# Stick-breaking attention on TensorE: the transposes of tile m-5 put ahead of the scores of tile m+3

## The chip, the cores and the metric

The program runs on one core of a Trainium2 chip. The metric is the device time of one execution in microseconds (us); the number that counts is the median over runs.

## What is computed

One inference step of an encoder layer for a prompt of 2048 rows and 32 sample rows, model width 1024. The part that matters here is the prompt's attention, 8 heads of width 64, strictly causal, with stick-breaking weights in place of a softmax:

```python
def stick_breaking_block(q_blk, q_pos, k, v, k_pos):
    z = jnp.einsum("bqhd,bkhd->bhqk", q_blk, k) * SB_SCALE
    mask = k_pos[None, :] < q_pos[:, None]
    log_1mb = jnp.where(mask, jax.nn.log_sigmoid(-z), 0.0)
    log_a = jax.nn.log_sigmoid(z) + lax.cumsum(log_1mb, axis=3, reverse=True) - log_1mb
    a = jnp.where(mask, jnp.exp(log_a), 0.0)
    return jnp.einsum("bhqk,bkhd->bqhd", a, v)
```

So the weight of key s for query t is sigmoid(z[t,s]) times the product of sigmoid(-z[t,j]) over the keys j between s and t. Ahead of it stand the conditioning, a layer norm, the projections and a pooling branch; behind it the output projection, two layer norms, a SwiGLU block and the sample rows.

## The kernel before

The kernel is one long program with hand-written queues for TensorE (`pe`), ScalarE (`act`), VectorE (`v`), GpSimd (`pool`) and the DMA queue (`sp`). Each engine runs its own list in order, and semaphores join them. No planner is in it: the order around the change is the order of the loops as they are written.

The attention stage goes over 8 heads. A head has ten units: query block b of 512 rows (0 to 3) against key block kc of 512 columns, from kc = b down to 0. The unit with kc == b is the diagonal one. With D for a diagonal unit and F for a full one, a head is D, D F, D F F, D F F F. A unit has four tiles, so there are 320 tiles; tile m = 4u + j belongs to unit u. On the score side, a tile is 128 query rows (j) by 512 key columns; in a diagonal unit tile j has only 128(j+1) columns. On the weight side, tile k = 4u + kt is one block of 128 keys (kt), transposed for up to four groups of query rows; in a diagonal unit kt has 4 - kt of them. These are the steps on a tile, with their lines:

- TensorE, `scores(m)`: two f16 matmuls into PSUM bank m % 4 (line 2211). From m = 4 on they wait until scan m-4 has freed the bank. In some units, j = 0 has also sixteen matmuls of a conditioning piece (line 2209).
- ScalarE, `plus(m)`, for a pair of tiles: the first sigmoid, into the buffer of weights C_A of the unit, of which there are three (line 1172). It waits for the scores of both tiles.
- ScalarE, `minus(m)`, for the same pair: the second sigmoid, in PSUM (line 1184).
- VectorE, `scan(m)`: the running product over the keys from right to left, out of PSUM into a row buffer (line 1707, on the diagonal 1704).
- GpSimd, `product(m)`: weights times the scan's result (line 880), on the diagonal behind a mask (line 876).
- TensorE, `turn_weights(k)`: up to four 128x128 f32 transposes into bank 4 + k % 2 (line 2234). With kt == 0 it waits for the product of the unit's last tile; from k = 2 on it waits until tile k-2 has been copied out.
- The copy of tile k out of PSUM into C_AT: ScalarE makes three of four (line 1195), VectorE the one with k % 4 == 1 (line 1725). VectorE's list has it at m = k + 6, behind scan(m), so the copy of tile 4i+1 stands behind scan 4i+7.
- TensorE, `weigh(k)`: weights times values, f32, into bank 6 or 7 (line 2250), for two tiles in every other pass of the loop.

At the end of each query block ScalarE (`head_low`, line 1202) and VectorE (line 1734) take the result out, and in odd heads GpSimd splits it into two f16 halves (lines 888 and 890, between two products). In even heads ScalarE and VectorE also split the pooling branch (`pool_high`, line 1210, and line 1742). ScalarE's list per unit is, with v the unit of the sigmoids: second sigmoid of tiles 2 and 3 of unit v-1, copy of tile 0 of unit v-2, first and second sigmoid of tiles 0 and 1 of unit v, copy of tile 2 of unit v-2, first sigmoid of tiles 2 and 3 of unit v, copy of tile 3 of unit v-2, and the second sigmoid of tiles 2 and 3 of unit v. `copied(k)` gives the semaphore and the count that stand for the copy of tile k:

```python
def copied(k):
    by_dve = (k + 3) // 4
    return (at_dve, by_dve) if k % 4 == 1 else (at_act, k + 1 - by_dve)
```

TensorE's list for the stage is the loop at line 2278: pass m has scores(m+3), then turn_weights(m-5), in every even pass weigh(m-8) and weigh(m-7), and at the very end the first matmuls of the output projection. Waits of the DMA queue on `z_mm` (scores done), `at_mm` (transposes done) and `av_mm` (weighed) release the loads of the next heads' q, k and v and of the conditioning pieces.

Of the kernel before, what the change touches and what calls it, by code (L numbers as in the profile page):

```python
# [57 lines left out]
def encoder_step(nc, x_prompt, x_sample, cache_k, cache_v, state_pool, c_prompt, c_sample,  # L58
# [5 lines left out]
    with ctx:  # L64
# [240 lines left out]
        NTILE = 4 * NU * NH  # L305

        def tile_of(m):
            u, j = m // 4, m % 4
            b, kc = UNITS[u % NU]
            return u, u // NU, b, kc, j, (j + 1) * P if kc == b else BLK  # L310
# [5 lines left out]
# [3 lines that stand above are left out]
# [1741 lines left out]
        def _(pe):  # L2060
# [136 lines left out]
            def scores(m):  # L2197
                u, h, b, kc, j, w = tile_of(m)
                e = h % 2
                qt = (4 * b + j) * P  # L2200
                if m % (4 * NU) == 0:
                    pe.wait_ge(head_in[e], 64 * (h // 2) + 64)
                if m >= 4:
                    pe.wait_ge(scan_set, m - 3)
                if j == 0 and u in ADA_AT:
                    pe.wait_ge(ada_in, 16 * (ADA_AT.index(u) + 1))
                    for d in range(KD):
                        at = TS * (d % 4)
                        pe.matmul(ps[at:at + TS, 0, 256:512], CT[:, d, :], C_ADA[:, d, :], start=(d < 4), stop=(d >= 4))
                for half in range(2):  # L2210
                    mm = pe.matmul(ps[:, m % 4, 0:w], C_Q[e][:, qt:qt + P], C_K[e][:, half, BLK * kc:BLK * kc + w],  # L2211
                                   start=(half == 0), stop=(half == 1))
                mm.then_inc(z_mm, 1)

            def turn_weights(k):
                u, h, b, kc, kt, w = tile_of(k)
                j0 = kt if kc == b else 0
                if kt == 0:
                    pe.wait_ge(prod_set, k + 4)
                if k >= 2:  # L2220
                    pe.wait_ge(*copied(k - 2))
                if kt == 1 and u in ADA_AT:
                    pe.wait_ge(mod_new, ADA_AT.index(u) + 1)
                    for q in range(2):
                        pe.matmul(ps[:, 4 + k % 2, 2 * q:2 * q + 2], MOD_ROW[:, q * P:(q + 1) * P], SEL,
                                  start=True, stop=True)
                if k == FIN_TURN:
                    pe.wait_ge(fin_max, 1)
                    pe.transpose(ps[0:5, 4 + k % 2, 0:P], small[:, 86:91], ident[:, :])
                if k == FIN_SPREAD:  # L2230
                    pe.wait_ge(fin_max, 2)
                    pe.matmul(ps[:, 4 + k % 2, 0:5], ones_r[0:5, :], TOP_DIAG[0:5, 0:5], start=True, stop=True)
                for j in range(j0, 4):
                    mm = pe.transpose(ps[:, 4 + k % 2, j * P:(j + 1) * P], C_A[u % 3][:, j, kt * P:(kt + 1) * P],  # L2234
                                      ident[:, :])
                mm.then_inc(at_mm, 1)

            def weigh(k):
                u, h, b, kc, kt, w = tile_of(k)
                e, r = h % 2, HD * (kt % 2)  # L2240
                j0 = kt * P if kc == b else 0
                pe.wait_ge(*copied(k))
                if k % (4 * NU) == 0:
                    pe.wait_ge(v_in[e], 16 * (h // 2) + 16)
                if kc == b and kt == 0 and 4 * h + b >= 2:
                    pe.wait_ge(o_scaled, 4 * h + b - 1)
                if kc == b and kt == 1:
                    pe.matmul(ps[HD:P, 6 + b % 2, 0:P], C_TRI[:, 0:HD], ident_b[:, :], start=True, stop=False,
                              skip_group_check=True)
                pe.matmul(ps[r:r + HD, 6 + b % 2, j0:BLK], C_V[e][:, 4 * kc + kt, :], C_AT[k % 4][:, j0:BLK],  # L2250
                          start=(kc == b and kt < 2), stop=(kc == 0 and kt >= 2),
                          skip_group_check=True).then_inc(av_mm, 1)

            def first_mix(k):
                pe.wait_ge(wo_hi, k + 1)
                pe.wait_ge(wo_lo, k + 1)
                if k == 0:
                    pe.wait_ge(o_split, 13)
                    pe.wait_ge(scan_set, NTILE - 2)
                for n in range(2):  # L2260
                    for xh, wh in TERMS:
                        mm = pe.matmul(ps[:, n, :], hidden_t[:, k, xh, tile_cols(0)], D_WO[k][:, wh, 512 * n:512 * (n + 1)],
                                       start=(k == 0 and (xh, wh) == (0, 0)),
                                       stop=(k == KD - 1 and (xh, wh) == TERMS[-1]))
                if k == KD - 1:
                    mm.then_inc(d_mm, 1)
# [9 lines left out]
            pe.wait_ge(mix_max, 2)  # L2276
            pe.matmul(ps[:, 7, 256:257], ones_r[0:1, :], TOP_DIAG[0:1, 0:1], start=True, stop=True).then_inc(mix_ar, 1)
            for m in range(NTILE + 7):
                if m + 3 < NTILE:
                    scores(m + 3)  # L2280
                if m == 5:
                    pe.wait_ge(kvt_out, 40)
                    pe.wait_ge(mix_set, 1)
                if 5 <= m < NTILE + 5:
                    turn_weights(m - 5)
                if m >= 8 and m % 2 == 0:
                    weigh(m - 8)
                    weigh(m - 7)
                if m >= NTILE + 1:
                    first_mix(m - NTILE - 1)  # L2290
# [258 lines left out]
```

## Time and profile before

| | |
|---|---|
| median of 3 runs | 2576.05 us (2575.98 to 2579.04) |
| the profiled execution's own time | 2579.84 us |
| its span | 2578.1 us |
| busy over the span | TensorE matmuls 2432.3 us (94%), weight loads 1347.5 (52%), VectorE 1415.5 (55%), ScalarE 1017.5 (39%), GpSimd 866.3 (34%) |
| TensorE clock granted, mean | 0.979 of full speed |
| attention stage | from about 484 to 1004 us of the span |

The profile is one execution, recorded by the hardware. The first view gives each engine's busy time; matmuls are pipelined, so neighbours overlap a little in it. A wait is idle time of an engine ahead of an instruction, put down to what released it. In a timeline, one line is one or several instructions of a kind in a row: start, duration up to the end of the last, engine, line of the program, operation, output and inputs, and in brackets the idle time before it. PE is TensorE's matmuls, PEld its weight loads, DVE is VectorE, ACT is ScalarE, POOL is GpSimd.

### The profile page before, as it was taken

The numbers are of one execution on the slowest core, as the hardware profiler recorded it, in microseconds if no ns is written. First come the engines' busy times: TensorE is split into PE (matmuls) and PEld (weight loads), VectorE is DVE, ScalarE is ACT, GpSimd is POOL, SyncE is SP. The second block draws the span as 40 slices with busy tenths as digits, with TensorE's granted clock in tenths as the row PEclk, the third lists the DMA queues.
The fourth block names the chain that finished last, engine by engine and source line by source line (L and its number), as shares of the span: only waits on it lengthen the run. The fifth ranks groups of instructions, "written<-read, shape, count | busy, mean of one in ns | idle before, by whom it ended". The sixth has DMA issues, their size and how long they took to land.

```text
span 2578.1 us, 36259 instructions
## 1 busy us (share of the span) xinstructions
PE 2432.3 (94%) x14328; PEld 1347.5 (52%) x14328; DVE 1415.5 (55%) x1861; ACT 1017.5 (39%) x1555; POOL 866.3 (34%) x1029
## 2 busy tenths in 40 slices
PE   4899899899999889999999999999999999999998
PEld 2445455444444444454565664345666544688733
DVE  4747665488888887889655553405333202433214
ACT  1522233499999994334444443102222200133200
POOL 1300000277777773324555556501111240111100
PEclk8899999899999999999999999999999999999999
DMA  7315868432332112222566666654544445566555
GB/s 250 101 50 172 279 235 270 127 99 82 99 97 68 34 66 98 78 98 77 166 198 195 190 204 224 237 183 155 162 161 135 136 135 181 160 222 200 187 164 167
DMA packets 216387, 395.63 MB, mean 153 GB/s; under 512 B 30189, under 2 KB 152365, under 8 KB 207642
## 3 DMA queue, kind: packets, MB, share of 16 engines
q1 hardware_dynamic: 199226, 331.45, 40.0%
q10 hardware_dynamic: 16992, 61.87, 7.8%
q8 instruction: 113, 1.85, 0.3%
q14 instruction: 56, 0.46, 0.1%
HBM read 302.97 MB, written 90.30 MB: 153 GB/s over the span
## 4 chain that ended last, share of the span: by engine, by line
PE 59%; DVE 9%; ACT 4%; DMA 3%; issue 3%; POOL 3%; SPq 0%; DVEq 0%; POOLq 0%; ACTq 0%
PE ps L2455 20%; PE ps L2495 15%; PE ps L2424 12%; PE ps L2359 3%; DMA dn_dram<-work 3%; DVE work L1707 2%; PE ps L2234 2%; PE ps L2250 2%; PE ps L2211 2%; POOL work L880 2%; ACT ps L1184 1%; ACT work L1172 1%; DVE work L1864 1%; DVE work L1704 1%; DVE work L1454 1%
## 5 line engine op out<-in xcount | busy, mean ns | idle before, releaser
L2455 PE MATMUL ps<-hidden_t,work 128*128 128x384 f16 (+1 forms) x3696 | 515.4, 303 | 2.2 <-ACT work L1305 1.1
L2495 PE MATMUL ps<-work 128*128 128x512 f16 x2244 | 472.6, 380 | 7.5 <-DVE work L1962 4.9
L2455 PEld LDWEIGHTS ps<-hidden_t,work 128*128 128x128 f16 x3696 | 361.3, 98 | 156.3 <-ACT work L1305 1.7
L2118 PE MATMUL ps<-hidden_t,work 128*128 128x416 f16 x1920 | 351.7, 343 | 14.3 <-DVE hidden_t L1472 9.8
L880 POOL TENSOR_TENSOR work<-work 128x512 f32<-128x512 f32 (+2 forms) x320 | 307.7, 964 | 134.4 <-DVE work L1707 76.4
L2424 PE MATMUL ps<-hidden_t,work 128*128 128x384 f16 x2112 | 347.4, 328 | 4.1 <-DVE work L1919 4.1
L2495 PEld LDWEIGHTS ps<-work 128*128 128x128 f16 x2244 | 206.6, 98 | 272.9 <-issue 28.6
L2424 PEld LDWEIGHTS ps<-hidden_t,work 128*128 128x128 f16 x2112 | 207.5, 98 | 144.2 <-issue 9.6
L2118 PEld LDWEIGHTS ps<-hidden_t,work 128*128 128x128 f16 x1920 | 189.7, 99 | 163.6 <-issue 16.1
L1707 DVE TENSOR_TENSOR_SCAN work<-ps,work 128x512 f32<-128x512 f32 x192 | 237.3, 1270 | 26.8 <-ACT ps L1184 25.7
L841 POOL TENSOR_TENSOR work<-work,col 128x1 f32<-128x1 f32 x68 | 33.2, 489 | 582.7 <-DVE work L1457 582.7
L945 POOL TENSOR_TENSOR work<-work 128x384 f16<-128x384 f32 (+1 forms) x88 | 75.2, 859 | 418.6 <-ACT work L1325 418.6
L2211 PE MATMUL ps<-work 128*128 128x512 f16 (+3 forms) x640 | 175.2, 357 | 37.1 <-DVE work L1707 29.6
L1979 DVE TENSOR_TENSOR work<-ps,work 128x1024 f32<-128x1024 f32 (+1 forms) x17 | 20.8, 1224 | 311.3 <-PE ps L2495 310.3
L2234 PE MATMUL ps<-ident,work 128*128 128x128 f32 x1088 | 178.9, 281 | 11.9 <-POOL work L880 6.9
L2234 PEld LDWEIGHTS ps<-ident,work 128*128 128x128 f32 x1088 | 132.5, 144 | 79.0 <-DVE work L1725 32.8
L1172 ACT ACTIVATE work<-ps,col 128x1024 f32<-128x1024 f32 (+1 forms) x160 | 165.5, 1034 | 8.5 <-PE ps L2211 6.9
L1184 ACT ACTIVATE ps<-ps,col 128x1024 f32<-128x1024 f32 (+1 forms) x160 | 161.3, 1008 | 2.2
L2250 PE MATMUL ps<-work 128*64 128x512 f32 (+3 forms) x640 | 160.8, 559 | 0.0
L1195 ACT ACTIVATE work<-ps,col 128x512 f32<-128x512 f32 (+2 forms) x240 | 148.5, 619 | 27.4 <-PE ps L2234 24.8
L2359 PE MATMUL ps<-work,hidden_t 128*128 128x512 f16 x720 | 159.2, 381 | 0.0
L1291 ACT ACTIVATE work<-ps 128x384 f32<-128x384 f32 (+1 forms) x44 | 19.6, 445 | 319.0 <-PE ps L2455 319.0
(243 smaller groups left out, 2691.6 us busy)
## 6 DMA issues: line engine op xcount, KB each, us to landing
work<-dn_dram ACTq DMA_DIRECT2D x96, 512.0 KB, 3.6
work<-gs_dram SPq DMA_DIRECT2D x88, 512.0 KB, 4.1
work<-gs_dram SPq DMA_DIRECT2D x44, 768.0 KB, 4.3
work<-in_w_ada SPq DMA_DIRECT2D x24, 1024.0 KB, 5.3
work<-in_w_gu SPq DMA_DIRECT2D x46, 512.0 KB, 7.0
work<-in_w_gu SPq DMA_DIRECT2D x22, 1024.0 KB, 6.0
gs_dram<-work SPq DMA_DIRECT2D x22, 1024.0 KB, 5.7
gs_dram<-work SPq DMA_DIRECT2D x66, 256.0 KB, 2.4
```

The source lines that it names most:

```text
L880: pool.tensor_tensor(a[:, 0:n], a[:, 0:n], PRJ[:, j, BLK * kc + 1:BLK * kc + n + 1], ALU.mult).then_inc(prod_set, 1)
L1172: act.activation(C_A[u % 3][:, j:j + 2, 0:n], ps[:, z:z + 2, 0:n], ACT.Sigmoid, scale=c1(C_Z + 2 * (h // 2) + 1)).then_inc(be_set, 1)
L1184: act.activation(ps[:, z:z + 2, 0:n], ps[:, z:z + 2, 0:n], ACT.Sigmoid, scale=c1(C_Z + 2 * (h // 2))).then_inc(sg_set, 1)
L1707: v.tensor_tensor_scan(row, ps[:, m % 4, w - 1::-1], row, PRJ[:, j, at + w:at + w + 1], ALU.mult, ALU.bypass).then_inc(scan_set, 1)
L2118: mm = pe.matmul(ps[:, blk, 0:PB], B_HL[s][:, wh * KD * P + k * P:wh * KD * P + (k + 1) * P], hidden_t[:, k, xh, PB * blk:PB * (blk + 1)], ...
L2211: mm = pe.matmul(ps[:, m % 4, 0:w], C_Q[e][:, qt:qt + P], C_K[e][:, half, BLK * kc:BLK * kc + w], start=(half == 0), stop=(half == 1))
L2234: mm = pe.transpose(ps[:, 4 + k % 2, j * P:(j + 1) * P], C_A[u % 3][:, j, kt * P:(kt + 1) * P], ident[:, :])
L2250: pe.matmul(ps[r:r + HD, 6 + b % 2, j0:BLK], C_V[e][:, 4 * kc + kt, :], C_AT[k % 4][:, j0:BLK], start=(kc == b and kt < 2), stop=(kc == 0 ...
L2359: mm = pe.matmul(ps[:, 2 * s + n, :], hidden_t[:, k, xh, tile_cols(t)], D_WO[k][:, wh, 512 * n:512 * (n + 1)], start=(k == 0 and (xh, wh) ...
L2424: mm = pe.matmul(ps[:, 2 * blk + w, 0:width], E_GHL[s][:, wh, w, k, :], hidden_t[:, k, xh, at:at + width], start=(k == 0 and (wh, xh) == ( ...
L2455: mm = pe.matmul(ps[:, bank, 0:n], E_GS[j % 2][:, GS_AT[q], wh, k, :], hidden_t[:, k0 + k, xh, at:at + n], start=(q in (1, 2, 5) and k == ...
L2495: mm = pe.matmul(ps[r:r + rows, 2 * slot + half, :], E_HID[:, j, xh, at:at + rows], E_DHL[slab_home(g)][:, wh, 512 * half:512 * (half + 1) ...
```

## The change

In each pass of the loop, `turn_weights(m - 5)` and the two waits at m == 5 now stand ahead of `scores(m + 3)`. Nothing else differs.

```diff
             for m in range(NTILE + 7):
-                if m + 3 < NTILE:
-                    scores(m + 3)
                 if m == 5:
                     pe.wait_ge(kvt_out, 40)
                     pe.wait_ge(mix_set, 1)
                 if 5 <= m < NTILE + 5:
                     turn_weights(m - 5)
+                if m + 3 < NTILE:
+                    scores(m + 3)
                 if m >= 8 and m % 2 == 0:
                     weigh(m - 8)
                     weigh(m - 7)
```

## Rows read from the trace of the kernel before

**Rows 1.** Busy time by engine over the attention stage, then clock, DMA share, GB/s.

```profile
484.00:1004.00 520.00, 469.50 (x2762) 223.50 (x2762) 436.05 (x524) 478.69 (x639) 367.19 (x478) 0.97 0.26 77
```

**Rows 2.** Who waited for whom, 490 to 990 us: us in total, times, longest.

```profile
PE ps L2211 <- DVE work L1707: 29.6, 53, 2.4
ACT work L1195 <- PE ps L2234: 19.2, 35, 3.0
PE ps L2234 <- POOL work L880: 6.9, 13, 2.1
ACT work L1172 <- PE ps L2211: 5.7, 14, 1.9
```

**Rows 3.** Timeline, VectorE: copies at three head boundaries, ten units apart.

```profile
612.31 0.73 DVE L1725 TENSOR_SCALAR work<-ps,col 128x512 f32<-128x512 f32 x1
...
675.11 0.73 DVE L1725 TENSOR_SCALAR work<-ps,col 128x512 f32<-128x512 f32 x1
...
735.91 0.73 DVE L1725 TENSOR_SCALAR work<-ps,col 128x512 f32<-128x512 f32 x1
```

**Rows 4.** Timeline, all engines, steps of units in head 3.

```profile
678.83 2.07 DVE L1704 TENSOR_TENSOR_SCAN work<-ps,work 128x384 f32<-128x384 f32 x2 [2.08 <-ACT ps L1184]
...
689.32 0.36 ACT L1195 ACTIVATE work<-ps,col 128x128 f32<-128x128 f32 x1
...
711.29 0.60 PE L2211 MATMUL ps<-work 128*128 128x512 f16 x2 [0.24 <-DVE work L1707]
...
711.93 1.11 ACT L1172 ACTIVATE work<-ps,col 128x1024 f32<-128x1024 f32 x1 [0.16 <-PE ps L2211]
...
714.31 0.65 PE L2234 MATMUL ps<-ident,work 128*128 128x128 f32 x4 [0.18 <-POOL work L880]
...
714.80 0.59 PE L2211 MATMUL ps<-work 128*128 128x512 f16 x2
...
718.44 1.11 ACT L1172 ACTIVATE work<-ps,col 128x1024 f32<-128x1024 f32 x1
...
719.44 0.69 ACT L1195 ACTIVATE work<-ps,col 128x512 f32<-128x512 f32 x1
...
720.01 1.10 ACT L1184 ACTIVATE ps<-ps,col 128x1024 f32<-128x1024 f32 x1
...
721.00 0.71 ACT L1195 ACTIVATE work<-ps,col 128x512 f32<-128x512 f32 x1
721.14 2.46 DVE L1707 TENSOR_TENSOR_SCAN work<-ps,work 128x512 f32<-128x512 f32 x2 [0.83 <-ACT ps L1184]
...
721.58 1.14 ACT L1172 ACTIVATE work<-ps,col 128x1024 f32<-128x1024 f32 x1
...
722.75 1.09 ACT L1184 ACTIVATE ps<-ps,col 128x1024 f32<-128x1024 f32 x1
...
723.56 0.61 DVE L1725 TENSOR_SCALAR work<-ps,col 128x384 f32<-128x384 f32 x1
...
724.23 0.33 PE L2234 MATMUL ps<-ident,work 128*128 128x128 f32 x1
```

**Rows 5.** Groups of instructions, 500 to 990 us: busy us, mean ns, idle before.

```profile
L1202 ACT ACTIVATE work<-ps 64x512 f32<-64x512 f32 x31 | 18.4, 594 | 0.8
L890 POOL TENSOR_TENSOR hidden_t<-work,hidden_t 128x512 f16<-128x512 f32 x15 | 17.4, 1163 | 1.2
L1210 ACT ACTIVATE hidden_t<-work,col 128x512 f16<-128x512 f32 x16 | 11.7, 732 | 0.0
```

**Rows 6.** Timeline, TensorE, the stage's first transposes.

```profile
497.01 1.09 PE L2234 MATMUL ps<-ident,work 128*128 128x128 f32 x4 [2.12 <-POOL work L880]
```

**Rows 7.** Timeline, TensorE, around two standstills.

```profile
874.59 0.39 PE L2211 MATMUL ps<-work 128*128 128x256 f16 x2 [1.30 <-DVE work L1707]
...
896.75 0.82 PE L2211 MATMUL ps<-work 128*128 128x384 f16 x2 [2.45 <-DVE work L1707]
...
900.07 1.97 PE L2250 MATMUL ps<-work 128*64 128x512 f32 x4
```

## The prediction, made before the changed kernel ran

> **What bounds the kernel now.** I read the stretches first: the attention loop takes about 520 of the 2578 us, and in it no engine is full: ScalarE 479 us, TensorE 470, VectorE 436, GpSimd 367 [rows 1]. A stage in which ScalarE stands at 92% and TensorE at 90% is held by loops that run through several engines, so the order inside each engine's stream counts. The waits come next: TensorE stands still for 29.6 us in 53 places in front of the scores, for a scan that frees a score bank, and ScalarE waits 19.2 us in 35 places for transposes (line 1195 for 2234); these are what the change could win [rows 2]. Then the timeline. VectorE's copy at line 1725 is issued once per unit of four tiles, right behind the unit's last scan, so its starts mark the end of each unit. From one head boundary to the next, ten units take 62.80 us in head 2 (even; it has the extra pool splits) and 60.80 us in head 3 (odd) [rows 3]. So a unit takes 6.1 to 6.3 us on average.
>
> In that timeline ScalarE runs nearly back to back. From one step's start to the next: second sigmoid to copy 0.99, copy to first sigmoid 0.58, first sigmoid to second 1.17, first sigmoid to copy 1.00, copy to second sigmoid 0.57 [rows 4]. One full unit is 0.99 + 0.58 + 1.17 + 0.99 + 0.58 + 1.00 + 0.57 = 5.88 us. Beside it stands a loop through three engines: last scan of unit v-1, scores of tile 3 of unit v (in the freed bank), sigmoids, scans of unit v. It is 0.10 + 0.64 + 1.00 + 0.57 + 1.13 + 2.42 = 5.86 us, in order: what is left of the scan when the copy's start is recorded and the release; scores to first sigmoid (711.29 to 711.93); first sigmoid to copy; copy to second sigmoid; second sigmoid to scans (720.01 to 721.14); two scans to the next copy (721.14 to 723.56). The two are level; that is the state the change meets.
>
> **The change, part by part.** Nothing is added or removed: same matmuls, same waits. Scores(m+3) and turn_weights(m-5) change places on TensorE, so whatever the transposes wait for, the scores now wait for too.
>
> Where the transposes are ready (three iterations in four), scores start later by one group of four transposes, 0.49 us from transposes to scores (714.31 to 714.80), and the transposes start earlier by the scores' time [rows 4]. For tiles 0 and 1 of a unit this lies beside ScalarE's work: their first sigmoid is issued behind the second sigmoid of the former pair and a copy, 0.99 + 0.58 = 1.57 us, and the two scores with two groups of transposes fit in. Cost nothing; if ScalarE ran dry there, 0.49 us a pair. TensorE's own work per unit is unchanged.
>
> The fourth iteration is m = 4i+8. Its transposes are of tile 4i+3 and wait for the copy of tile 4i+1, the one that VectorE makes (copied(k-2), k % 4 == 1). VectorE issues it only behind scan 4i+7. The scores behind them, tile 4i+11, need just that scan. So where scores used to start at the scan's end, they now wait for the copy and the transposes. The trace shows the pieces: copy to transposes 0.67 for the 384-wide copy (723.56 to 724.23) [rows 4], and 0.12 more for the full one, 0.73 long against 0.61, so 0.79 [rows 3]; transposes to scores 0.49. Today scores stand ahead of them, and at 711.93 the first sigmoid starts 0.64 behind its scores, after 0.16 of waiting: no slack [rows 4]. Behind the waiting transposes are queued the scores, the two weigh steps and, through the scores, the sigmoid pair, the scans and GpSimd's product.
>
> New loop, full unit with full units before it: 0.79 + 0.49 + 0.64 + 1.00 + 0.57 + 1.13 + 2.42 = 7.04 us. The other three cases: if unit v-1 is on the diagonal its last two scans take 2.07 instead of 2.46, so 6.65. If unit v-2 is on the diagonal, the copy is the 384-wide one (0.67), one transpose is left (0.20, an estimate between nothing and 0.49) and ScalarE's copy is 0.33 shorter (0.36 against 0.69, so 0.24), together 6.30; if both, 5.91 [rows 4].
>
> A head is D D F D F F D F F F (D diagonal, F full). The loop by unit: 7.04, 6.65, 5.91, 6.30, 6.65, 6.30, 7.04, 6.65, 6.30, 7.04, in all 65.9 us. ScalarE's path goes above it only in the third unit, where a head_low (0.59 long, 0.62 taken) joins: 5.88 + 0.62 - 0.33 = 6.17, so 66.1 for an odd head. Even heads have five pool_high steps on ScalarE (0.73 long, about 0.61 each in the row) [rows 5]; two fall in the eighth unit, 5.88 + 1.22 = 7.10 against 6.65, and the ninth gains 0.1 to 0.2: 66.7. Against the measured 60.8 and 62.8 that is +5.3 and +3.9 us, four heads of each: +36.8 us.
>
> Other bound: the same rule, the larger of loop and ScalarE path per unit, used on the kernel before gives about 58.8 and 61.0, that is 2 us a head less than measured, for waits outside both. If all of these remain, the difference is 7.3 and 5.7 a head, +52 us. If the transposes' earlier start takes back ScalarE's waits for them, at most 19.2 us [rows 2], it is +18 (+19 with the stage's start, below). I stay near the middle row, since seven units in ten are held by the new loop, in which small waits elsewhere have room.
>
> At the start of the stage scores(8) go behind the first transposes, which waited 2.12 us for GpSimd [rows 6], and behind the waits on kvt_out and mix_set at m == 5: between 0 and 2.12 us; I take 1.4, once. The end is untouched, since no scores are issued from m = 317 on. SP's loads that wait on z_mm are issued up to 1.2 us later and are used a unit or more later: nothing. Everything behind the stage shifts as a whole.
>
> A rule weighed: the rows say that ScalarE has the highest share in this stage, 92% [rows 1]. The Trainium skill, "Perfetto Trace Analysis", section Identifying the Most-Contended Engine, has the busiest engine as the one that matters. Since the change leaves ScalarE's work alone, by that rule the sum would be nothing; by the chain of rows it is +37. It stands below as the rival "hidden".
>
> **Sum.** +36.8 + 1.4 = +38 us on the profiled execution, whose own time is 2579.84 us, 1.5‰ above the median of the three runs, 2576.05. The stage is the same in both, so 2576 + 38 = 2614 us.
>
> **The rivals.** *Faster.* The place is TensorE's 29.6 us in front of scores: ready transposes now fill it, and ScalarE's 19.2 us of waits for transposes go [rows 2]. Price: up to -19 us, 2557 us. It decides if the copy of tile 4i+1 is done before TensorE comes to the transposes of 4i+3. Against it: that copy is recorded behind the last scan in each unit I looked at. For it: only if much slack lies between scores and sigmoid at m = 4i+8, and 711.29 to 711.93 shows none. 8%.
>
> *Hidden.* ScalarE's path stays the limit and the delay of the scores lies beside it: within 5 us of 2576. For: ScalarE at 92%. Against: 7.04 against 5.88, an excess of 1.16 us that nothing on ScalarE covers. That the swap changes nothing at all would look alike. 5%.
>
> *GpSimd too.* Transposes of tile 0 wait for the product of tile 3 of the same unit, and now scores of the next unit wait with them. In odd heads a split of two steps (the second 1.16 us, the pair about 1.8) stands before a product in 15 to 16 places [rows 5], and the transposes waited 6.9 us for GpSimd already [rows 2]. Price on top: 15 x 1.8 = 27 us, 2641 us. Against it: the new loop leaves about 1.5 us there. 8%, and it ends the range above.
>
> *Clock.* After a standstill of 2.45 us the 384-wide scores at 896.75 took 0.82 us, where 512-wide ones take 0.60 at 711.29, and weigh steps still took 1.97 at 900.07: 5.3 us at the lower of the two levels (1.2 of 2.4 GHz); after 1.30 us at 874.59 the 256-wide ones took 0.39 [rows 4, 7]. The new order gives TensorE a gap of about 1.4 us in each full unit. If the clock fell there in the three longest units of each head (24), with 5.3 us at half rate each, 2.6 us more work against 1 us of room: 24 x 1.6 = +38 more, 2652 us. The Trainium skill, "TensorE: Matmul & The Clock Gate", section A second HAM failure mode: psum-queue depth-cycling, tells of short frequent standstills that make the clock swing; this trace shows 1.30 us gaps that don't. 5%.
>
> **How the numbers follow.** Forecast 74%, rivals 8, 5, 8 and 5. The range leaves out faster, hidden and clock, 18 in 100: low end +19 us, 2595; high end GpSimd's 2641. 0.2%, 5 us, is what a measurement of this kernel can tell from no change. Faster 0.08, same 0.05, slower 0.87.
>
> **What would show it.** In the profile after: the stage some 38 us longer; per unit 6.3 to 7.0 us between starts of line 1725, 66 us a head, with odd and even heads nearly equal; scores at m = 4i+8 start about 1.2 us behind the copy's start and not at its start; ScalarE waits at line 1172 for line 2211, once per unit about 1 us, 60 to 90 us in all where it was 5.7 [rows 2]; its waits at line 1195 shrink; TensorE's wait at line 2234 for 1725 becomes the longest of the stage. Wrong if line 1172 waits little, if units keep their 6.1 us, or if the granted clock of the stage drops below 0.9.

## The result and the profile after

The changed kernel takes 2613.73 us (median of 4 runs, 2611.56 to 2615.26), the kernel before on the same chip 2577.07 us. The ratio is 1.0147, with a 95% interval of 1.0134 to 1.0159: slower by 36.7 us. The forecast was 2614 us.

The attention stage over the whole engine set, same columns as [rows 1]:

```profile
484.00:1041.00 557.00, 474.80 (x2760) 219.83 (x2759) 436.33 (x524) 480.34 (x639) 367.98 (x478) 0.97 0.25 71
```

The stage ends about 37 us later, and every engine has the work it had: ScalarE 480 us against 479, VectorE 436 against 436. ScalarE's share is now 86% where it was 92%. The granted clock is 0.97 in both. So 37 us of standing still were added.

The waits, 490 to 990 us (us in total, times, longest), beside [rows 2]:

```profile
ACT work L1172 <- PE ps L2211: 55.3, 62, 3.8
PE ps L2234 <- DVE work L1725: 52.1, 66, 1.9
PE ps L2234 <- POOL work L880: 8.1, 12, 3.4
PE ps L2211 <- DVE work L1707: 5.1, 8, 2.3
ACT work L1195 <- PE ps L2234: 2.9, 2, 2.3
```

The two waits that the change could win are nearly gone: TensorE's wait ahead of its scores falls from 29.6 to 5.1 us, ScalarE's for transposes from 19.2 to 2.9. In their place TensorE stands 52.1 us at its transposes for VectorE's copy, in 66 places, which is close to once in a unit, and ScalarE waits 55.3 us for scores, where it waited 5.7.

VectorE's copies, which mark the ends of units, at the same head boundaries as [rows 3] and for six units inside head 3:

```profile
620.72 0.72 DVE L1725 TENSOR_SCALAR work<-ps,col 128x512 f32<-128x512 f32 x1
...
687.40 0.72 DVE L1725 TENSOR_SCALAR work<-ps,col 128x512 f32<-128x512 f32 x1
...
700.64 0.61 DVE L1725 TENSOR_SCALAR work<-ps,col 128x384 f32<-128x384 f32 x1
707.14 0.59 DVE L1725 TENSOR_SCALAR work<-ps,col 128x384 f32<-128x384 f32 x1
712.96 0.73 DVE L1725 TENSOR_SCALAR work<-ps,col 128x512 f32<-128x512 f32 x1
719.99 0.61 DVE L1725 TENSOR_SCALAR work<-ps,col 128x384 f32<-128x384 f32 x1
726.64 0.73 DVE L1725 TENSOR_SCALAR work<-ps,col 128x512 f32<-128x512 f32 x1
...
753.48 0.72 DVE L1725 TENSOR_SCALAR work<-ps,col 128x512 f32<-128x512 f32 x1
```

Head 2 takes 66.68 us (620.72 to 687.40) and head 3 66.08 (687.40 to 753.48); before, 62.80 and 60.80. The third unit of head 3, which ends at 707.14, took 6.50, the next ones 5.82, 7.03 and 6.65.

The new loop, in the timeline of all engines, for a diagonal unit (the seventh of head 3):

```profile
726.64 0.73 DVE L1725 TENSOR_SCALAR work<-ps,col 128x512 f32<-128x512 f32 x1
...
727.42 0.66 PE L2234 MATMUL ps<-ident,work 128*128 128x128 f32 x4 [1.05 <-DVE work L1725]
...
727.91 0.59 PE L2211 MATMUL ps<-work 128*128 128x512 f16 x2
...
728.54 1.11 ACT L1172 ACTIVATE work<-ps,col 128x1024 f32<-128x1024 f32 x1 [1.50 <-PE ps L2211]
...
729.56 0.68 ACT L1195 ACTIVATE work<-ps,col 128x512 f32<-128x512 f32 x1
...
730.13 1.09 ACT L1184 ACTIVATE ps<-ps,col 128x1024 f32<-128x1024 f32 x1
...
731.25 2.07 DVE L1704 TENSOR_TENSOR_SCAN work<-ps,work 128x384 f32<-128x384 f32 x2 [2.97 <-ACT ps L1184]
```

From start to start: copy to transposes 0.78, to scores 0.49, to the first sigmoid 0.63, to ScalarE's copy 1.02, to the second sigmoid 0.57, to the scans 1.12, and 1.99 to the next copy at 733.24: 6.60 us. ScalarE stands 1.50 us for its scores, and the scans 2.97 us for ScalarE.

### The profile page after: what moved, and what is told of

Read it like the earlier page. It is cut to its first block, busy times and chain, and to the rows that moved or that the text cites. A ratio compares the mean times of both kernels' runs of the same rounds, so it can differ in the third digit from the quotient of the medians.

```text
span 2612.6 us, 36259 instructions
## 1 busy us (share of the span) xinstructions
PE 2440.5 (93%) x14328; PEld 1346.6 (52%) x14328; DVE 1418.6 (54%) x1861; ACT 1018.9 (39%) x1555; POOL 866.8 (33%) x1029
## 4 chain that ended last, share of the span: by engine, by line
PE 57%; DVE 10%; issue 4%; ACT 4%; DMA 3%; POOL 3%; DVEq 0%; SPq 0%; POOLq 0%; ACTq 0%
PE ps L2455 19%; PE ps L2495 15%; PE ps L2424 12%; PE ps L2359 3%; DVE work L1707 3%; DMA dn_dram<-work 3%; PE ps L2250 2%; ACT ps L1184 2%; POOL work L880 2%; PE ps L2234 2%; DVE work L1725 1%; PE ps L2211 1%; DVE work L1864 1%; ACT work L1172 1%; DVE work L1704 1%
## 5 line engine op out<-in xcount | busy, mean ns | idle before, releaser
L2118 PE MATMUL ps<-hidden_t,work 128*128 128x416 f16 x1920 | 351.9, 344 | 12.5 <-DVE hidden_t L1472 8.2
L2234 PE MATMUL ps<-ident,work 128*128 128x128 f32 x1088 | 188.5, 290 | 70.9 <-DVE work L1725 60.9
L2234 PEld LDWEIGHTS ps<-ident,work 128*128 128x128 f32 x1088 | 120.7, 144 | 232.4 <-DVE work L1725 95.2
```

Of the source, the lines that this page charges most:

```text
L2118: mm = pe.matmul(ps[:, blk, 0:PB], B_HL[s][:, wh * KD * P + k * P:wh * KD * P + (k + 1) * P], hidden_t[:, k, xh, PB * blk:PB * (blk + 1)], ...
```

## The experiments

All were timed beside the kernel before, so each is given as its ratio to that, with the 95% interval; 0.1% is 2.6 us. The theory: the cost is the loop that leads through VectorE's copy, closed in passes m % 4 == 0 alone. The rivals: each pass pays for the delay of its scores; or GpSimd's product, for which the transposes of tile 4i wait; or TensorE's order by itself.

**Which of the four passes costs.** In the first run the transposes come first only where they wait for VectorE's copy, in the second only in the other three passes.

```diff
             for m in range(NTILE + 7):
-                if m + 3 < NTILE:
+                swap = m % 4 == 0
+                if m + 3 < NTILE and not swap:
                     scores(m + 3)
...
                     turn_weights(m - 5)
+                if m + 3 < NTILE and swap:
+                    scores(m + 3)
```

> Only the passes m % 4 == 0 have the transposes first (those of tile 4i+3, which wait for VectorE's copy); the other three have the scores first as before. Theory loop (scores wait for VectorE's copy): the whole cost is here, 2608 to 2616 us, 66 us a head. Rival spread (each pass of the loop delays its scores by the transposes' 0.49 us and pays a like share): a quarter of the cost, about 2586. Rival GpSimd (the transposes of tile 0 wait for the product, scores behind them): nothing of it is here, about 2577.

> The reverse: passes m % 4 == 1, 2, 3 have the transposes first, m % 4 == 0 has the scores first. Theory loop: no cost, 2565 to 2580 us, with a little to win from earlier transposes (ScalarE's waits at line 1195, 19 us before, should fall under 8). Rival spread: three quarters of the cost, about 2604. Rival GpSimd: nearly all of it, 2605 to 2613.

The fourth pass alone: 2610.49 us, 1.0127 (1.0113 to 1.0141), and 66.47 and 65.62 us for heads 2 and 3. The other three: 2592.24 us, 1.0048 (1.0035 to 1.0060). Most of the cost is where the theory has it, and the rival with equal shares is out: its quarter would have been 2586. But the other three passes, which the theory had at nothing, cost 12 us by themselves, and the band expected for them (2565 to 2580 us) is missed. The two parts, 33 and 12 us, come to more than the whole, 37, so in the changed kernel the smaller is largely hidden beside the larger: its heads 2 and 3 are only 0.21 and 0.46 us longer than those of the fourth-pass run. The waits of the second run, 490 to 990 us:

```profile
PEld ps L2234 <- POOL work L880: 52.0, 49, 2.0
ACT work L1172 <- PE ps L2211: 32.2, 55, 2.4
...
ACT work L1195 <- PE ps L2234: 7.1, 12, 2.3
```

ScalarE waits less for transposes, as expected, but 32.2 us for scores where it waited 5.7. The three passes were then run one by one, with `swap = m % 4 == 1`, `== 2` and `== 3`.

> Transposes first only in passes m % 4 == 1: those of tile 4i, which wait for GpSimd's product of tile 4i+3, stand ahead of scores 4(i+2). The three passes together cost 14 us. If GpSimd's product is what costs there: most of it here, 2586 to 2593 us. If each of the three passes just pays its 0.49 us delay where ScalarE runs dry: about a third, 2583.

> Transposes first only in passes m % 4 == 2 (tile 4i+1 ahead of scores 4i+9; these transposes wait for ScalarE's copy of tile 4i-1). If GpSimd's product is the cost: 2575 to 2582 us. If each pass pays its delay: about 2583.

> Transposes first only in passes m % 4 == 3 (tile 4i+2 ahead of scores 4i+10). The scores that hold the pair's sigmoid are those of tile 4i+11, one pass later, so the delay is free, and ScalarE's copy of tile 4i+2 gets its transposes earlier: 2565 to 2577 us, ScalarE's waits at line 1195 under 10 us. If each pass pays its delay: about 2583.

| transposes first only in | median, us | ratio | ScalarE for scores | ScalarE for transposes |
|---|---|---|---|---|
| m % 4 == 1 | 2584.35 | 1.0024 (1.0013 to 1.0035) | 11.9 us | 21.0 us |
| m % 4 == 2 | 2581.12 | 1.0016 (1.0007 to 1.0025) | 11.3 us | 17.3 us |
| m % 4 == 3 | 2572.10 | 0.9979 (0.9969 to 0.9989) | 12.5 us | 13.3 us |

The waits of the run with m % 4 == 1 show how its transposes of tile 4i stand for GpSimd (weight loads of line 2234, 48 times):

```profile
PEld ps L2234 <- POOL work L880: 51.2, 48, 2.0
...
PE ps L2234 <- POOL work L880: 15.6, 15, 4.2
ACT work L1172 <- PE ps L2211: 11.9, 29, 1.9
```

The weight loads waited 11.2 us there in the kernel before, and the transposes themselves 6.9 [rows 2].

The waits of the run with m % 4 == 3:

```profile
ACT work L1195 <- PE ps L2234: 13.3, 31, 2.3
ACT work L1172 <- PE ps L2211: 12.5, 25, 2.4
```

Six and four us slower, and five faster. The first is below the 2586 to 2593 us expected if GpSimd's product held most of the cost, and nearer to the 2583 us of an equal share: it has about half of the 12 us, and its interval (3 to 9 us) leaves open which of the two it is. The second is at the upper end of the 2575 to 2582 us expected if GpSimd's product is the cost, and 2 us under the 2583 of an equal share, so it tells little. The third shows a pass in which the swap pays. The reading, from the order of the loop: its transposes feed a copy that ScalarE is about to make, and its scores, tile 2 of a unit, can be late without harm, since the sigmoid needs those of tile 3 too. ScalarE's waits for transposes fall from 19.2 to 13.3 us, though not under the 10 us expected. One by one the three give +5 us and together +12; why they don't add up was not settled.

**VectorE's copy moved to an earlier place.** VectorE stands idle ahead of scan 4i+6; the copy of tile 4i+1 is put there, in the new order and, as a control, in the old one.

```diff
             for m in range(NTILE + 10):
+                if 6 <= m < NTILE + 5 and m % 4 == 2:
+                    at_copy(m - 5)
                 if m < NTILE:
                     scan(m)
...
-                if 6 <= m < NTILE + 6 and m % 4 == 3:
-                    at_copy(m - 6)
```

> The changed order in all passes, but VectorE makes the copy of tile 4i+1 ahead of scan 4i+6, into the time in which it waits for ScalarE, and not behind scan 4i+7. Theory loop: the scores of tile 4i+11 then wait for the scan alone, the loop is back at 5.9 us a unit, 2560 to 2582 us. Rival spread: stays at 2605 to 2614. Rival that the copy in its new place delays the scans by its whole 0.65 us: 2577 + 52 x (share of units) = up to 2629.

> The kernel before with the same move of VectorE's copy. Theory loop: in the old order no scores wait for this copy, so 2570 to 2580 us; the control for the run with the early copy in the new order. If the move by itself gave or cost much (over 10 us either way), the gain of that run would not be the loop's.

Both expectations failed: 2620.36 us, 1.0160 (1.0146 to 1.0173), and 2656.64 us, 1.0300 (1.0286 to 1.0314). The control had to stay level and lost 78 us, so this pair can't test the theory. The waits of the control, 490 to 990 us:

```profile
DVE work L1725 <- PE ps L2234: 94.6, 49, 4.6
ACT work L1195 <- PE ps L2234: 82.6, 93, 2.8
PE ps L2211 <- DVE work L1707: 67.8, 84, 3.1
```

At that place the tile's transposes have not been made. VectorE waited 94.6 us at the copy, where the changed kernel has 1.5, and the scans, which everything else needs, stood behind it. The idle time ahead of scan 4i+6 was time in which the copy's input did not exist. In the new order the same move costs far less, 3 to 7 us over the changed kernel; ScalarE's waits for transposes are 9.7 us there, and 82.6 here.

**The copy between the last two scans.** Here its input is there. It lies in the way of scan 4i+7 in either order, so either order should have the same loop, and the scores should wait for a scan alone. In the new order the swap is kept in passes m % 4 == 0 only.

```diff
             for m in range(NTILE + 10):
+                if 6 <= m < NTILE + 6 and m % 4 == 3:
+                    at_copy(m - 6)
                 if m < NTILE:
                     scan(m)
...
-                if 6 <= m < NTILE + 6 and m % 4 == 3:
-                    at_copy(m - 6)
```

> Transposes first only in passes m % 4 == 0, and VectorE makes the copy of tile 4i+1 between scans 4i+6 and 4i+7. The copy then still lies in the way of the scan that frees the bank, 0.65 us, but the transposes' 0.49 us run beside scan 4i+7. Theory loop: about 6.5 us for a full unit, 2588 to 2604 us, and within 8 us of the same move in the old order. Rival (the transposes in front cost by themselves): 2605 to 2616.

> The old order with the same move of the copy: the copy now stands in the way of scan 4i+7 here too, so the old order gets the same loop. Theory loop: 2588 to 2604 us, slower than the kernel before by 12 us or more. If the order on TensorE is what costs and not the copy's place in the loop: 2572 to 2582 us.

With transposes first 2591.05 us, 1.0044 (1.0031 to 1.0058), with scores first 2595.81 us, 1.0059 (1.0047 to 1.0071). The same move takes 19 to 21 us off the one (1.0127 before it) and adds 15 to 16 to the other, and both land within the expected band, 5 us apart, with intervals that overlap. Once the copy stands in the loop whatever TensorE does, TensorE's order in this pass has no cost that these runs can tell. The timeline of the run with transposes first:

```profile
704.91 0.61 DVE L1725 TENSOR_SCALAR work<-ps,col 128x384 f32<-128x384 f32 x1
705.43 2.45 DVE L1707 TENSOR_TENSOR_SCAN work<-ps,work 128x512 f32<-128x512 f32 x2
...
706.08 0.49 PE L2234 MATMUL ps<-ident,work 128*128 128x128 f32 x3
...
706.76 0.61 PE L2211 MATMUL ps<-work 128*128 128x512 f16 x2 [0.19 <-DVE work L1707]
```

The copy is over 1.2 us before the scores, and the transposes (706.08) run beside the scan. The scores start at 706.76 behind a scan and no longer behind transposes that waited.

**A shorter copy.** VectorE copies only the last 128 columns of its tiles, so part of the weights is missing from the output; these kernels serve for their time alone. The copy falls to 0.33 us, from 0.72 in full units and 0.60 on the diagonal. That is 3.5 us a head, somewhat more than the 3.2 that the expectation took.

```diff
-                v.tensor_scalar(C_AT[k % 4][:, j0:BLK], ps[:, 4 + k % 2, j0:BLK], c1(C_SMIX), None,
+                v.tensor_scalar(C_AT[k % 4][:, BLK - P:BLK], ps[:, 4 + k % 2, BLK - P:BLK], c1(C_SMIX), None,
                                 ALU.mult).then_inc(at_dve, 1)
```

> The changed order; VectorE's copy of tile 4i+1 takes only the last 128 columns of the tile (the rest of C_AT is left as it was, so part of the weights is missing from the output). The copy gets 0.36 us shorter in full units, 0.25 on the diagonal, 3.2 us a head. Theory loop (the copy stands in the loop that sets the time): 2587 to 2592 us. Rival that the cost is TensorE's order or delay by itself and the copy only happens to stand there: 2608 to 2614.

> Transposes first only in passes m % 4 == 0, and VectorE's copy takes the last 128 columns alone (part of the weights is missing from the output). The new order's other three passes, which cost up to 14 us and may have set a floor under the run with the narrow copy in all passes, are out. Theory loop: 2.6 us a head less than with the full copy, 2588 to 2593 us. If the cost is TensorE's order by itself: 2605 to 2612.

> The control: the old order with the narrow copy (same part of the output missing). VectorE has 3.2 us a head less to do, but in the old order no scores wait for the copy: theory loop 2570 to 2578 us. If it falls as far as the new order does (14 us or more, under 2563), VectorE's load and not the wait is what the narrow copy takes away.

| kernel | full copy | narrow copy |
|---|---|---|
| old order | 1 | 0.9983 (0.9974 to 0.9991) |
| transposes first, m % 4 == 0 | 1.0127 (1.0113 to 1.0141) | 1.0039 (1.0026 to 1.0052) |
| transposes first, all passes | 1.0147 (1.0134 to 1.0159) | 1.0081 (1.0068 to 1.0094) |

The same 28 us or so of copying less (3.5 us a head) is worth 4 us in the old order (2575.06 us, in the expected band), 17 in the changed kernel and 23 where only the fourth pass is swapped. The middle row is the clean one, 2590.52 us, as expected: four fifths of the shortening come back as time, so the copy stands in the loop that sets it. The changed kernel gave less than expected, 2599.74 against 2587 to 2592 us. It stands 11 us above the middle row, which fits the 12 us that the other three passes cost in their own run: with the large loop shortened, their delays come out beside it. In the fourth-pass kernel with the narrow copy the chain reads as before, only shorter:

```profile
645.37 0.34 DVE L1725 TENSOR_SCALAR work<-ps,col 128x128 f32<-128x128 f32 x1
...
645.76 0.33 PE L2234 MATMUL ps<-ident,work 128*128 128x128 f32 x1 [0.37 <-DVE work L1725]
645.93 0.59 PE L2211 MATMUL ps<-work 128*128 128x512 f16 x2
...
646.68 1.11 ACT L1172 ACTIVATE work<-ps,col 128x1024 f32<-128x1024 f32 x1
```

From copy to transposes 0.39 us, where the 384-wide copy had 0.67 [rows 4].

## Why the prediction was right

*The mechanism.* The scores of tile 4i+11 wait for VectorE's copy of tile 4i+1 through the transposes of tile 4i+3. The trace after shows it once a unit, the fourth-pass run shows 33 of the 37 us there, and the shorter copy and the moved copy change the time as a member of the loop must.

*The terms of the loop.* Full copy to transposes 0.79 forecast, 0.78 found; transposes to scores 0.49 and 0.49; scores to sigmoid 0.64 and 0.63. A single transpose to scores, estimated at 0.20, was 0.16 (707.79 to 707.95). The forecast counts a unit from scans to scans, so it has 5.91, 6.30, 6.65 and 6.30 us for the third to the sixth unit. The rows above go from copy to copy, and there the 2.07 us of a diagonal unit's scans falls in that unit and not in the next: the same terms give 6.30, 5.91, 7.04 and 6.30, and found were 6.50, 5.82, 7.03 and 6.65. The sum of a head is the same either way. The heads: 66.1 forecast and 66.08 found for the odd one, 66.7 and 66.68 for the even one. That match to a tenth has luck in it. ScalarE's path, 0.26 us longer there, puts the third unit at 6.56; the sixth was 0.35 us over, which comes from the other three passes, since it took 6.23 in the fourth-pass run; the rest were up to 0.1 under.

*The sum over eight heads* has luck in it too. Numbered from 0, heads 1 to 5 grew by 5.3 (odd) and 3.9 us (even), as forecast. Head 0 has no copy to wait for in its first two units, and I had counted them: from its second copy (506.52 before, 507.88 after) to its end (551.51 and 554.64) it grew by 1.8 us, and not by 3.9. Heads 6 and 7 grew by 4.5 and 6.3 us, 0.6 and 1.0 more than forecast, and why is not settled. Up to its last copy the stage is 37.5 us longer in the two profiles, but their spans differ by 34.5 (2578.1 and 2612.6 us). So what stands behind the stage was 3 us shorter and did not just shift. The four runs of each kernel spread by 3 to 4 us, and this may be no more than that.

*Taking the larger of two paths.* I set the rule's head against the measured one, and so left out the 2 us a head of waits that the same rule missed in the kernel before. The result bears that out, and the bound of +52 us would have been wrong. That these waits had room beside the longer loop is the reading; no run takes them apart.

*"Cost nothing" for the passes with ready transposes.* This step failed, taken by itself. I took it that ScalarE had 1.57 us of other work there. By themselves these passes cost 12 us, about half of it in the pass whose transposes, of tile 4i, wait for GpSimd. In the changed kernel it hardly shows, 37 against 33 us. That the longer loop of the fourth pass leaves room for it is the likely reason, and is not shown by a run of its own. The sum was right since this term is hidden, not since it is nothing; the rival "GpSimd too" named the place, but TensorE's wait for GpSimd at its transposes is 8.1 us in the changed kernel, where it was 6.9.

*The start of the stage.* The first transposes start at 497.13 in place of 497.01, and the second of VectorE's copies at 507.88 in place of 506.52: 1.4 us forecast, 1.36 found. The size is right and the path is not. I had scores(8) wait as the first transposes wait for GpSimd, and so they do: they start at 498.01 in place of 493.85. But the first sigmoid of tiles 8 and 9 waits for scores(9) too, and those stood behind these transposes already, at 497.89:

```profile
497.13 1.09 PE L2234 MATMUL ps<-ident,work 128*128 128x128 f32 x4 [3.38 <-POOL work L880]
498.01 1.06 PE L2211 MATMUL ps<-work 128*128 128x512 f16 x2
498.86 0.85 PE L2234 MATMUL ps<-ident,work 128*128 128x128 f32 x3
499.50 1.06 PE L2211 MATMUL ps<-work 128*128 128x512 f16 x2
```

What came between is scores(8) and the second group of transposes, 1.49 us from 498.01 to 499.50, with the granted clock at 0.50 (496 to 500 us, before and after). The sigmoid starts at 500.60 in place of 498.99. That it equals the 1.4 taken out of 0 to 2.12 is luck.

*The rivals.* "Faster" was right on what can be won, since both waits it named nearly went, 24 and 16 us, and wrong on their worth: neither stood in what set the time any more. The swap in one pass of four does win, by 0.21%. "Hidden" is out, and with it the reading by shares: ScalarE had 92% and its work stayed as it was, and yet the time went up. "Clock": the standstill of the unit shown is 1.05 us and the clock of the stage stays at 0.97, as 1.30 us had let expect [rows 7].

*The marks.* Scores start 1.27 us behind the copy's start where 1.2 was forecast. ScalarE's wait at line 1172 was forecast at 60 to 90 us and is 55.3 up to 990 us and 58.4 up to 1027, a little short.

The fastest kernel of this study is the old order with the swap in passes m % 4 == 3 alone, 0.9979 of the kernel before (0.9969 to 0.9989).

## What to carry to other kernels

When two steps change places in an in-order queue, write down for each what it waits for: the one moved back takes over all waits of the one in front. Look for the instance in the repeating pattern that waits for something issued late, price the loop it closes from start-to-start times, and compare it with the loops that hold the time now. A swap that hurts as a whole can pay in one pass out of four, so take the passes apart. Before a step is moved into an engine's idle time, look whether its input is there by then.

## What the runs showed that I had not expected

VectorE's idle time ahead of scan 4i+6 looked free and was the costliest of the places tried for the copy: 78 us in the old order. Costs of the same swap also don't add up: 33 and 12 us by themselves made 37 together, while +6, +4 and -5 us for three passes made +12.
